# Three paired-attention stages: where unit weights are loaded, and the order of copies, exponentials and the closing projection

## The chip, the cores and the metric

One core of one Trainium2 chip runs the whole program in one launch. The metric is the device time in microseconds (us) of an execution; three executions of the kernel before took 2148.76, 2148.96 and 2149.0 us, so the median is 2148.96 us. The core has a matrix engine (TensorE, PE in the rows; its weight loads are PEld), VectorE (DVE), ScalarE (ACT), GpSimd (POOL) and SyncE (SP, which here only issues DMAs). Data lie in an on-chip memory of 128 partitions, matrix products land in eight PSUM banks of 128 x 512 floats.

## The reference

The reference runs two blocks on 512 tokens of width 1024, all in float32. The first is a layer norm, a gated mixer with two attentions, a norm, a mixture of 32 experts (top 4) and a norm. The second is a mixer of a sparse attention ("nsa"), a stick-breaking attention and a gated recurrence, then a norm. Three attentions matter here, cut to their core:

```python
# 1. differential attention, 4 heads, two score maps per head        (stage "diff")
s = einsum('bhqcd,bhkcd->cbhqk', q_blk, k);  p = softmax(where(allowed, s + alibi, -inf))
a = p[0] - lam * p[1];                       out = a @ v
# 2. chunk band attention, 8 heads with a relative bias                (stage "band")
p = softmax(where(valid, q_blk @ kb.T + bias, -inf));  out = p @ vb
# 3. nsa attention, 6 heads in 2 groups                                (stage "nsa")
p_c = masked_softmax(q @ kc.T * scale + bias_c)      # 31 compressed keys
p_s, p_w = ...                                       # selected blocks, and a window
out = g0 * (p_c @ vc) + g1 * (p_s @ vs) + g2 * (p_w @ vw)
```

Queries and keys come from products such as h @ w_in of 512 tokens by 1024 features.

## The kernel before, in words

The program is a row of stages with a barrier of all engines between them, so a stage that ends earlier moves all that follows. Three stages share one code, `heads_stage` (L638): "diff" (about 37 to 144 us of the span), "band" (174 to 268 us) and "nsa" (1779 to 1880 us).

A **unit** is a pair of score maps computed together: two halves m = 0, 1 of 64 feature rows each. diff and band have 4 units with 4 **items** each, one per block of 128 queries, with 128, 256, 384 and 512 keys. nsa has 3 units of 9 items: place 0 is the small item (31 compressed keys for all queries, 124 columns per half), then two items per query block (places 1 to 8: 128, 128, 256, 256, ... 512, 512 keys). Items are numbered t = 0, 1, ...; `items.place(t)` is the place in the unit and `items.closes(t)` marks the last place.

Every matrix is kept as a rounded upper part (a ScalarE cast, `upper_part`, L757) and a remainder (`split_lower`, L139), and a product takes three matmuls (L134 to L136). While unit u is worked on, the **projection** of unit u + 1 (queries and keys in diff and band, queries alone in nsa) is cut into pieces and spread over the items (`projection`, L724): 12 matmuls per item in diff and band, 3 per item at places 0 to 7 in nsa. In nsa, unit 0 is projected by the stage before.

For item t the engines run in lock step over semaphores. TensorE (L439): scores of t (L452), a share of the next projection, transposes of item t - 2 (L465, or L473 with the two halves apart), weighted values of item t - 3 (L487 or L492). VectorE (L498): scores plus bias with the row maximum (L511), then the normalisation of item t - 1 (L542 to L556), then at a closing item the copy of the next keys (`next_keys`, L803, L806), which a following unit's scores wait for. ScalarE (L570): exponentials of t (L582, L579 for the small item), the next queries' copy out of PSUM (`next_queries`, L776, L780), the copies of the transposed item t - 2 out of PSUM (L594 in diff, L599 in band and nsa), and then `weights`, the casts for a later unit. The copies free the banks that the next transposes write, half by half.

In nsa three more things are done beside. SyncE loads, first of all (`following`, L686), 2 MB of weights for the stick-breaking stage into `ahead`, then the query weights of unit 1 (`nsa_raw`) and of unit 2 (`nsa_q_raw`), two DMAs of 256 KB each with rows of 64 floats (L2125). ScalarE waits for unit 1's weights before it begins item 0 (L797). Four casts of `ahead` into `sb_up_qk` go out in units 1 and 2 (places 2 and 4, L774), and GpSimd takes their four remainders `ahead_lower` (L709); GpSimd also takes the remainders of the units' weights (L703) in all three stages.

## Time and profile before

| | |
|---|---|
| median of three executions | 2148.96 us |
| profiled execution | 2153.57 us |
| its span, first to last instruction | 2151.8 us |
| TensorE busy in the span | 90% |
| VectorE, ScalarE, GpSimd busy | 75%, 57%, 14% |
| first, second, third attention stretch (69 to 147, 188 to 270, 1780 to 1880 us) | TensorE busy 68.55 of 78, 74.49 of 82, 77.32 of 100 us |
| mean granted TensorE clock | 0.954 of full |

The profile is of one execution and has its own time; 1.8 us of it lie outside the span. In a row in order of time the first number is the start in us from the span's start, the second the length in us (of the whole group, where xN instructions stand in one row), and the brackets say how long the engine had been idle before it and what ended that. The middle of the span, about 430 to 1680 us, is the mixture of experts, which this change does not touch.

### The profile page before, as it was taken

To read this page: it belongs to the slowest core of one execution; us is meant where nothing else is said; L and a number is where in the kernel's file an instruction comes from. 1 tells how busy PE (TensorE), PEld (TensorE's weight loads), DVE (VectorE), ACT (ScalarE), POOL (GpSimd) and SP (SyncE) were. 2 spreads that over 40 slices of the span, in tenths; PEclk is the share of its full clock that TensorE was granted. 3 is DMA by queue.
4 is the path that set the end of the run, shared out by engine and by line. 5 is a ranking of instruction groups with operands and counts; after the bars stand their busy time and mean duration, and the time that the engine had idled before them with its cause. 6 is when DMAs were issued, how large, how long until landed. Compare 5 with 4: busy or idle time off the path is not lost. (4 is left out here: it accounts for less than half of the span.)

```text
span 2151.8 us, 28805 instructions
## 1 busy us (share of the span) xinstructions
PE 1945.5 (90%) x10052; PEld 1559.5 (72%) x10052; DVE 1610.0 (75%) x1815; ACT 1226.9 (57%) x1311; POOL 310.8 (14%) x176
## 2 busy tenths in 40 slices
PE   4988899974999999999999999999998497889998
PEld 3766678753788888888888888888886384576876
DVE  5363451457899999999999999999999434634786
ACT  3343532323677777777777777777776134642551
POOL 0202043101021212121111111111111000100000
PEclk9999999986999999999999999999999698999999
DMA  6222144445899999999999999999997352011122
GB/s 206 59 78 79 30 104 110 154 147 223 314 367 395 376 390 376 384 377 392 375 390 374 389 378 388 377 383 383 381 382 285 94 139 59 5 46 59 50 70 79
DMA packets 201612, 518.95 MB, mean 241 GB/s; under 512 B 21974, under 2 KB 81502, under 8 KB 201196
## 3 DMA queue, kind: packets, MB, share of 16 engines
q1 hardware_dynamic: 191212, 482.68, 60.3%
q0 software_dynamic: 9504, 34.61, 6.1%
q8 instruction: 41, 0.67, 0.1%
q10 hardware_dynamic: 832, 0.80, 0.1%
q14 instruction: 23, 0.19, 0.0%
HBM read 494.41 MB, written 29.41 MB: 243 GB/s over the span
## 5 line engine op out<-in xcount | busy, mean ns | idle before, releaser
L1759 ACT CAST moe_upper<-piece 128x2048 fp32r<-128x2048 f32 x384 | 734.1, 1914 | 284.7 <-PE bank L1691 270.1
L1839 DVE TENSOR_TENSOR piece_lower<-piece,moe_upper 128x2048 fp32r<-128x2048 f32 x384 | 870.1, 2286 | 30.0 <-ACT moe_upper L1759 30.0
L1689 PE MATMUL bank<-moe_upper,x_hi 128*128 128x512 f32 x1536 | 621.4, 405 | 2.5 <-DVE x_hi L1833 2.5
L1691 PE MATMUL bank<-moe_upper,x_hi 128*128 128x512 f32 x1536 | 607.1, 395 | 0.0
L1690 PE MATMUL bank<-piece_lower,x_hi 128*128 128x512 f32 x1536 | 602.5, 392 | 0.0
L1689 PEld LDWEIGHTS bank<-moe_upper,x_hi 128*128 128x128 f32 x1536 | 290.9, 189 | 67.8 <-DVE piece_lower L1839 2.9
L1690 PEld LDWEIGHTS bank<-piece_lower,x_hi 128*128 128x128 f32 x1536 | 290.7, 189 | 62.9
L1691 PEld LDWEIGHTS bank<-moe_upper,x_hi 128*128 128x128 f32 x1536 | 290.4, 189 | 62.6
L1643 POOL DMA_INDIRECT mixed<-moe_y,moe_dst x32 | 104.8, 3275 | 27.5 <-issue 27.5
L136 PE MATMUL bank<-x_hi,ahead_lower 128*128 128x512 f32 x256 | 102.1, 399 | 0.0
L1641 POOL COPY moe_dst<-row 128x1 uint32 (+1 forms) x32 | 6.9, 217 | 611.6 <-ACT moe_y L1748 611.6
L1633 POOL COPY moe_tok<-token 128x1 uint32 (+1 forms) x34 | 30.3, 890 | 341.5 <-DMA mixed<-moe_y,moe_dst 279.1
L1126 DVE TENSOR_TENSOR merge_tmp<-merge_sig,bank 128x512 f32<-128x512 f32 x8 | 5.5, 688 | 81.8 <-PE bank L136 81.5
L1635 POOL DMA_INDIRECT ahead<-h,moe_tok x34 | 61.0, 1795 | 32.5 <-issue 32.5
L300 PE MATMUL bank<-const,xs 128*128 128x128 f32 x96 | 20.3, 397 | 43.7 <-DVE xs L230 24.0
L136 PEld LDWEIGHTS bank<-x_hi,ahead_lower 128*128 128x128 f32 x256 | 49.3, 193 | 10.9
L135 PE MATMUL bank<-ahead_lower,x_hi 128*128 128x512 f32 (+1 forms) x140 | 55.8, 399 | 0.0
L134 PE MATMUL bank<-x_hi,merge_upper 128*128 128x512 f32 x128 | 50.6, 396 | 4.1 <-DVE ahead_lower L141 4.1
L300 PEld LDWEIGHTS bank<-const,xs 128*128 128x128 f32 x96 | 18.4, 213 | 47.8 <-DVE xs L230 44.8
L1828 DVE TENSOR_TENSOR moe_a<-moe_u,moe_sg 128x512 f32<-128x512 f32 x64 | 44.3, 693 | 10.6 <-issue 10.2
L135 PE MATMUL bank<-x_lo,merge_upper 128*128 128x512 f32 x128 | 50.4, 394 | 0.0
L1748 ACT ACTIVATE moe_y<-bank,slot_weight 128x512 f32<-128x512 f32 x64 | 40.2, 679 | 15.1 <-PE bank L1691 15.1
(571 smaller groups left out, 3051.5 us busy)
## 6 DMA issues: line engine op xcount, KB each, us to landing
piece<-in_w_exp_in_dram SPq DMA_DIRECT2D x256, 1024.0 KB, 7.7
piece<-in_w_exp_out_dram SPq DMA_DIRECT2D x128, 1024.0 KB, 9.6
ahead<-in_w_in_dram SPq DMA_DIRECT2D x19, 512.0 KB, 4.9
ahead<-in_w_in_dram SPq DMA_DIRECT2D x3, 2048.0 KB, 8.1
ahead<-in_w_in_dram SPq DMA_DIRECT2D x4, 1536.0 KB, 7.1
merge_raw<-in_w_in_dram SPq DMA_DIRECT2D x8, 512.0 KB, 5.5
ahead<-in_w_out_dram SPq DMA_DIRECT2D x2, 2048.0 KB, 7.9
out_w<-in_w_out_dram SPq DMA_DIRECT2D x2, 2048.0 KB, 8.3
```

The source lines that it names most:

```text
L134: nc.tensor.matmul(out, lhs.hi, rhs.hi, start=start, stop=False)
L135: nc.tensor.matmul(out, lhs.hi, rhs.lo, start=False, stop=False)
L136: return nc.tensor.matmul(out, lhs.lo, rhs.hi, start=False, stop=stop)
L1635: nc.gpsimd.indirect_dma_start(out=rows_in[p][:, :], out_offset=None, in_=k.h1[:, :], in_offset=bass.IndirectOffsetOnAxis(ap=tok[:, p:p + ...
L1643: nc.gpsimd.indirect_dma_start(out=k.mixed[:, :], out_offset=bass.IndirectOffsetOnAxis(ap=dst[:, 0:1], axis=0), in_=y[:, :], in_offset=Non ...
L1689: nc.tensor.matmul(to, hi[:, f, :], upper[u][:, t, cols], start=f == 0 and not biased, stop=False)
L1690: nc.tensor.matmul(to, hi[:, f, :], lower[s][:, t, cols], start=False, stop=False)
L1691: done = nc.tensor.matmul(to, lo[:, f, :], upper[u][:, t, cols], start=False, stop=f == NK - 1)
L1748: nc.scalar.activation(y[:, 512 * c:512 * c + 512], k.bank[4 + c][:, :], ACT.Copy, scale=r.slot_weight[:, ds(j, 1)]).then_inc(y_sb, 1)
L1759: nc.scalar.copy(upper[h % SPLIT][:, :, :], ring[s][:, :, :]).then_inc(hi_ready, 1)
L1828: nc.vector.tensor_tensor(a2[half][:, :], u2[half][:, :], sg2[half][:, :], ALU.mult) .then_inc(a_ready, 1)
L1839: nc.vector.tensor_tensor(lower[s][:, :, :], ring[s][:, :, :], upper[h % SPLIT][:, :, :].bitcast(F32), ALU.subtract).then_inc(lo_ready, 1)
```

## The change

It has eight parts.

1. TensorE: at a closing item the share of the next projection is issued ahead of the scores, not behind (diff and band; in nsa the closing place has no share).
2. VectorE: `next_keys` at a closing item stands ahead of that item's bias, not behind the normalisation.
3. ScalarE: for item t the copies of item t - 2 come first, then the next queries, then the exponentials, then `weights`.
4. nsa, SyncE: the query weights of unit 1 are loaded first, and `following` comes after them.
5. nsa, ScalarE: the cast of unit 1's weights is not waited for before item 0 but stands behind its exponential.
6. nsa, TensorE: the projection of unit 1 leaves places 0 and 1 free (`LATE = 2`) and has its 8 pieces at places 2 to 7, as 1, 1, 2, 1, 1, 2.
7. nsa: the four remainders `ahead_lower` are VectorE's, in units 1 and 2 at places 3 and 5, behind the normalisation.
8. GpSimd keeps the remainders of the units' weights alone.

```diff
 (attention_pe)
+            if items.closes(t):
+                projection(u + 1, items.place(t))
             if t >= 2:
                 pe.wait_ge(b["biased"], at + t - 1)
...
-            projection(u + 1, items.place(t))
+            if not items.closes(t):
+                projection(u + 1, items.place(t))
 (attention_dve)
+            if items.closes(t):
+                next_keys(u + 1)
             dve.wait_ge(b["scored"], at + t + 1)
...
-        if t < N and items.closes(t):
-            next_keys(items.unit(t) + 1)
+        if t < N:
+            other(items.unit(t), items.place(t))
 (attention_act: the block of the exponentials and next_queries moves behind the copies)
         if t < N:
+            next_queries(items.unit(t) + 1, items.place(t))
+            it = items.item(t)
+            e = b["e"][:, t % RING, :, 0:it["keys"]]
+            act.wait_ge(b["biased"], at + t + 1)
...
+            last.then_inc(b["exped"], 1)
             weights(items.unit(t) + 2, items.place(t))
 (heads_stage, sync)
-            if beside is not None:
-                following(sp)
             for u in range(done, units):
+                if beside is not None and u == 2:
+                    following(sp)
 (heads_stage, gpsimd)
-            if beside is not None:
-                for m in range(4):
...
-                    split_lower(nc.gpsimd, k.ahead[:, :, part], beside[:, :, part], k.ahead_lower[:, :, part])
 (heads_stage, tensor)
+                late = LATE if beside is not None and u == 1 else 0
+                step, steps = step - late, STEPS - late
+                if u < units and 0 <= step < steps:
+                    for n, c in PIECES[step * len(PIECES) // steps:(step + 1) * len(PIECES) // steps]:
                         project(u, n, c)
 (heads_stage, scalar)
             def weights(u, step):
+                if beside is not None and u == 2 and step == 0:
+                    upper_part(1, 0)
...
-            for n in range(projections):
-                upper_part(1, n)
+            if beside is None:
+                for n in range(projections):
+                    upper_part(1, n)
 (heads_stage, vector)
+            def remainders(u, step):
+                if beside is not None and u >= 1 and step in (3, 5):
+                    m = 2 * (u - 1) + (step - 3) // 2
+                    part = slice(P * m, P * m + P)
+                    dve.wait_ge(beside_hi, m + 1)
+                    split_lower(nc.vector, k.ahead[:, :, part], beside[:, :, part], k.ahead_lower[:, :, part])
```

What moves in the instruction order, at the three places that matter. Lines of the changed kernel are a few higher: L452 is L454 there, L465 is L468, L487 is L490, L582 is L603, L579 is L600, L599 is L592, L594 is L587, L780 is L783, L760 is L761, L2125 is L2136, L473 is L476, L556 is L561.

TensorE, diff, the closing item of unit 2 (scores 128x512) before: scores, then the first of the four pieces of unit 3's projection.

```order
L487 MATMUL bank<-v,diff_pt 128x128 [waits attention_copied]
L487 MATMUL bank<-v,diff_pt 128x128 x3
L452 MATMUL bank<-diff_heads_kt,diff_heads_q 128x512 [waits attention_biased]
L452 MATMUL bank<-diff_heads_kt,diff_heads_q 128x512
L134 MATMUL bank<-x_hi,v_upper 128x512
L135 MATMUL bank<-x_lo,v_upper 128x512
L136 MATMUL bank<-x_hi,ahead_lower 128x512
L134 MATMUL bank<-x_hi,v_upper 128x512
```

After: the end of the same projection, the scores, the transposes of item 9 and values of item 8 and the first scores of unit 3.

```order
L135 MATMUL bank<-x_lo,v_upper 128x512
L136 MATMUL bank<-x_hi,ahead_lower 128x512
L454 MATMUL bank<-diff_heads_kt,diff_heads_q 128x512 [waits attention_biased]
L454 MATMUL bank<-diff_heads_kt,diff_heads_q 128x512
L468 MATMUL bank<-const,diff_scores 128x128 [waits attention_copied,attention_normed]
L468 MATMUL bank<-const,diff_scores 128x128
L490 MATMUL bank<-v,diff_pt 128x128 [waits attention_out_copied,attention_copied]
L454 MATMUL bank<-diff_heads_kt,diff_heads_q 128x128 [waits attention_biased,units_evacuated]
```

The twelve projection matmuls are now ahead of the closing scores, and nothing long is left between those scores and the next unit's first ones.

SyncE at the start of nsa, before:

```order
L683 UNCONDITIONAL_BRANCH [waits barrier_Pool_Activation_PE_DVE_SP_release]
L310 DMA ahead<-in_w_in_dram 128x8x512
L2125 DMA nsa_raw<-in_w_in_dram 128x8x64 x2
L2125 DMA nsa_q_raw<-in_w_in_dram 128x8x64 [waits units_projected]
L2125 DMA nsa_q_raw<-in_w_in_dram 128x8x64
```

After:

```order
L687 UNCONDITIONAL_BRANCH [waits barrier_Pool_Activation_PE_DVE_SP_release]
L2136 DMA nsa_raw<-in_w_in_dram 128x8x64 x2
L310 DMA ahead<-in_w_in_dram 128x8x512
L2136 DMA nsa_q_raw<-in_w_in_dram 128x8x64 [waits units_projected]
L2136 DMA nsa_q_raw<-in_w_in_dram 128x8x64
```

The two DMAs of unit 1's weights now stand ahead of the 2 MB.

ScalarE at the start of nsa, before: items 0, 1 and 2, then the first copies.

```order
L780 ACTIVATE nsa_heads_q<-bank 128x512
L760 CAST nsa_upper<-nsa_raw 128x1024 [waits units_w1_in]
L579 ACT_TABLE_LOAD
L579 ACTIVATE nsa_scores<-nsa_scores 128x2x124 [waits attention_biased]
L582 ACTIVATE nsa_scores,nsa_l<-nsa_scores,nsa_nm 128x128 [waits attention_biased]
L582 ACTIVATE nsa_scores,nsa_l<-nsa_scores,nsa_nm 128x128
L582 ACTIVATE nsa_scores,nsa_l<-nsa_scores,nsa_nm 128x128 [waits attention_biased]
L582 ACTIVATE nsa_scores,nsa_l<-nsa_scores,nsa_nm 128x128
L599 COPY nsa_pt<-bank 31x512 [waits attention_transposed] x2
L582 ACTIVATE nsa_scores,nsa_l<-nsa_scores,nsa_nm 128x256 [waits attention_biased]
L582 ACTIVATE nsa_scores,nsa_l<-nsa_scores,nsa_nm 128x256
```

After:

```order
L783 ACTIVATE nsa_heads_q<-bank 128x512
L600 ACT_TABLE_LOAD
L600 ACTIVATE nsa_scores<-nsa_scores 128x2x124 [waits attention_biased]
L761 CAST nsa_upper<-nsa_raw 128x1024 [waits units_w1_in]
L603 ACTIVATE nsa_scores,nsa_l<-nsa_scores,nsa_nm 128x128 [waits attention_biased]
L603 ACTIVATE nsa_scores,nsa_l<-nsa_scores,nsa_nm 128x128
L592 COPY nsa_pt<-bank 31x512 [waits attention_transposed] x2
L603 ACTIVATE nsa_scores,nsa_l<-nsa_scores,nsa_nm 128x128 [waits attention_biased]
L603 ACTIVATE nsa_scores,nsa_l<-nsa_scores,nsa_nm 128x128
L592 COPY nsa_pt<-bank 128x128 [waits attention_transposed] x2
L603 ACTIVATE nsa_scores,nsa_l<-nsa_scores,nsa_nm 128x256 [waits attention_biased]
L603 ACTIVATE nsa_scores,nsa_l<-nsa_scores,nsa_nm 128x256
```

The cast that waits for the load (`units_w1_in`) has gone behind the first exponential, and each pair of copies is now ahead of the exponentials of the item two later.

## Rows read from the trace of the kernel before

**Rows 1.** Third attention stage, busy: PE, PEld, DVE, ACT, POOL; then clock, DMA share, GB/s.

```profile
1780.00:1880.00 100.00, 77.32 (x588) 50.04 (x588) 60.36 (x195) 58.28 (x166) 14.20 (x6) 0.90 0.12 32
```

**Rows 2.** Order of time, start of the third stage: start us, length us, engine, line.

```profile
1779.69 0.38 SPq L310 DMA_DIRECT2D ahead<-in_w_in_dram  x1
1780.13 4.44 SPq L2125 DMA_DIRECT2D nsa_raw<-in_w_in_dram  x2
1783.32 0.42 DVE L521 TENSOR_TENSOR nsa_scores<-nsa_scores,nsa_heads_small_m 128x248 f32<-128x248 f32 x1
1790.02 1.04 ACT L760 CAST nsa_upper<-nsa_raw 128x1024 fp32r<-128x1024 f32 x1 [9.70 <-DMA nsa_raw<-in_w_in_dram]
1791.15 2.34 POOL L141 TENSOR_TENSOR nsa_raw_lower<-nsa_raw,nsa_upper 128x1024 fp32r<-128x1024 f32 x1 [106.66 <-ACT nsa_upper L760]
1793.55 0.79 PE L134 MATMUL bank<-x_hi,nsa_upper 128*128 128x512 f32 x1 [11.25 <-POOL nsa_raw_lower L141]
1795.12 0.80 PE L452 MATMUL bank<-ks_t,nsa_heads_q 64*128 64x128 f32 x4
```

**Rows 3.** One tile, the query weights: issues (ns min/median/max) and landings.

```profile
L1966 SPq DMA_DIRECT2D nsa_q_raw<-in_w_in_dram x2: 1817/1898/1979, 1727.6 to 1729.7; - x2
DMA to landing us min/median/max: 4.3/6.0/6.2
```

**Rows 4.** Waits in the third stage: who for whom, us in total, times, longest.

```profile
PE bank L452 <- ACT nsa_heads_q L780: 5.4, 3, 2.3
PE bank L473 <- DVE nsa_scores L556: 3.5, 4, 1.8
PE bank L473 <- ACT nsa_pt L599: 2.7, 5, 1.2
```

**Rows 5.** Order of time, third stage: queries at a unit change, GpSimd beside VectorE.

```profile
1815.75 0.88 PE L492 MATMUL bank<-nsa_pt,vs 128*64 128x128 f32 x12
1817.57 0.57 ACT L780 ACTIVATE nsa_heads_q<-bank 128x512 f32<-128x512 f32 x1
1832.64 0.73 DVE L556 TENSOR_SCALAR nsa_scores<-nsa_scores,nsa_l,gates 128x256 f32<-128x256 f32 x2
1834.95 2.37 POOL L141 TENSOR_TENSOR ahead_lower<-ahead,sb_up_qk 128x1024 fp32r<-128x1024 f32 x1 [3.61 <-ACT sb_up_qk L774]
1835.22 2.57 DVE L556 TENSOR_SCALAR nsa_scores<-nsa_scores,nsa_l,gates 128x256 f32<-128x256 f32 x2
```

**Rows 6.** One line, the remainders on VectorE in the stage before: ns min/median/max.

```profile
L141 DVE TENSOR_TENSOR ahead_lower<-ahead,sb_up_qk x3: 1219/1220/1225, 1726.4 to 1728.7; 128x1024 fp32r<-128x1024 f32 x3
```

**Rows 7.** Waits in the first and in the second stage, as in rows 4.

```profile
PE bank L452 <- DVE diff_heads_kt L806: 2.6, 4, 1.0
...
PE bank L452 <- DVE band_heads_kt L806: 1.0, 2, 0.9
```

**Rows 8.** Order of time, first stage, change to its last unit.

```profile
124.12 0.50 PE L134 MATMUL bank<-x_hi,v_upper 128*128 128x512 f32 x1
124.24 0.69 DVE L511 CUSTOM_DVE_ANT_0 diff_scores<-bank,band_table 128x512 f32<-128x512 f32 x1 [0.31 <-PE bank L452]
126.28 0.62 DVE L548 SCALAR_TENSOR_TENSOR diff_scores<-diff_scores,diff_l 128x384 f32<-128x384 f32 x1
126.99 0.38 PE L465 MATMUL bank<-const,diff_scores 128*128 128x128 f32 x2
128.35 0.55 PE L465 MATMUL bank<-const,diff_scores 128*128 128x128 f32 x3
```

**Rows 9.** Order of time, end of the second stage.

```profile
259.28 0.72 ACT L582 ACTIVATE band_scores<-band_scores,band_nm 128x512 f32<-128x512 f32 x1 [2.04 <-DVE band_nm L511]
259.40 0.75 DVE L554 TENSOR_SCALAR band_scores<-band_scores,band_l 128x384 f32<-128x384 f32 x2
260.70 0.62 ACT L599 COPY band_pt<-bank 128x256 f32<-128x256 f32 x2
261.19 1.37 PE L473 MATMUL bank<-const,band_scores 128*128 128x128 f32 x6 [2.58 <-ACT band_pt L599]
```

More of the change, by code:

```diff
@@ L495, in attention_pe, with attention_dve @@
             last.then_inc(b["weighed"], 1)
-def attention_dve(nc, dve, k, items, b, next_keys, copy_out, ordered):
+def attention_dve(nc, dve, k, items, b, next_keys, copy_out, ordered, other):
     N, at = items.n, b["at"]
@@ L573, in attention_act @@
     for t in range(N + VALUE_LAG + 1):
-        if t < N:
-            it = items.item(t)
-            e = b["e"][:, t % RING, :, 0:it["keys"]]
-            act.wait_ge(b["biased"], at + t + 1)
-            if it["small"] is not None:
-                last = nc.scalar.activation(e, e, ACT.Exp)
-            else:
-                for m in range(2):
-                    last = nc.scalar.activation(e[:, m, :], e[:, m, :], ACT.Exp, bias=b["nm"][:, t % RING, m:m + 1],
-                                                scale=-1.0, accum_out=b["l"][:, t % RING, m:m + 1])
-            last.then_inc(b["exped"], 1)
-            next_queries(items.unit(t) + 1, items.place(t))
         n = t - TURN_LAG
@@ L601, in attention_act @@
         if t < N:
+            next_queries(items.unit(t) + 1, items.place(t))
+            it = items.item(t)
+            e = b["e"][:, t % RING, :, 0:it["keys"]]
+            act.wait_ge(b["biased"], at + t + 1)
+            if it["small"] is not None:
+                last = nc.scalar.activation(e, e, ACT.Exp)
+            else:
+                for m in range(2):
+                    last = nc.scalar.activation(e[:, m, :], e[:, m, :], ACT.Exp, bias=b["nm"][:, t % RING, m:m + 1],
+                                                scale=-1.0, accum_out=b["l"][:, t % RING, m:m + 1])
+            last.then_inc(b["exped"], 1)
             weights(items.unit(t) + 2, items.place(t))
@@ L632 @@
 UNIT_SEMS = ("w0_in", "w1_in", "w_hi", "w_split", "projected", "evacuated", "v_hi", "v_lo", "v_ps", "v_sb")
-FIRST_BANK = 3
+FIRST_BANK, LATE = 3, 2
 def heads_stage(nc, name, k, load, projections, items, values, q, copy_out, upper_out=None, keys=None, following=None,
@@ L724, in projection @@
             def projection(u, step):
-                if u < units and step < STEPS:
-                    for n, c in PIECES[step * len(PIECES) // STEPS:(step + 1) * len(PIECES) // STEPS]:
+                late = LATE if beside is not None and u == 1 else 0
+                step, steps = step - late, STEPS - late
+                if u < units and 0 <= step < steps:
+                    for n, c in PIECES[step * len(PIECES) // steps:(step + 1) * len(PIECES) // steps]:
                         project(u, n, c)
@@ L819, in _ @@
             next_keys(0)
-            attention_dve(nc, dve, k, items, b, next_keys, copy_out, keys is not None and upper_out is not None)
+            def remainders(u, step):
[4 more added lines that the diff above has]
+                    split_lower(nc.vector, k.ahead[:, :, part], beside[:, :, part], k.ahead_lower[:, :, part])
+            attention_dve(nc, dve, k, items, b, next_keys, copy_out, keys is not None and upper_out is not None, remainders)
     k.attention.counted(scored=items.n, out_copied=2 * units)
```

2 lines of the change are left out of this document (removed).

## The prediction

> **What bounds the kernel now.** I read the stretch of each attention stage first, since the change lies in these three alone, and barriers put whatever they gain or lose into the total. In the first two TensorE is busy for nine tenths of the time (the small table ahead), so they have little to give; in the third it is busy for 77.32 of 100 us [rows 1]. The order of time there shows one hole: TensorE ended the first scores at 1782.30 (1793.55 less the 11.25 in brackets) and stood until GpSimd's remainder of unit 1's weights was ready [rows 2]. Behind it is a chain: SyncE issued the 2 MB `ahead` first, then the two DMAs of `nsa_raw`; ScalarE waited for them until 1790.02 with nothing else done, cast for 1.04, GpSimd took 2.34. The waits of that stage name the rest: TensorE waited 5.4 us in three goes for the queries, 3.5 in four for VectorE's normalisation, 2.7 in five for ScalarE's copies of the transposes [rows 4]. In diff and band it waited 2.6 and 1.0 us for the copied keys [rows 7]. Elsewhere in these stages TensorE is the bound, so what is moved beside it costs nothing until it lets TensorE wait.
>
> **The load of unit 1's weights (parts 4 to 6).** The two DMAs now go out at the stage's start, 1779.7. In the stage before, an issue of this shape took 1.82 to 1.98 us, and the landings lay 4.3 to 6.2 us behind their issue [rows 3]. So the second goes out at 1781.6 and lands between 1785.9 and 1787.8. I take 1786.2, near the short end, because nothing stands ahead of it in its queue. ScalarE has by then the first exponential behind it (its input is ready at 1783.74, rows 2) and casts at once. Cast and remainder with their hand-overs took 3.53 us (1790.02 to 1793.55), so the projection can start at 1789.7, against 1793.55: 3.8 us sooner (2.2 to 4.1 by the landings; 0 if the load is no sooner at all). Meanwhile TensorE has computed the scores of items 1 and 2, which before came behind the hole: 0.80 for one [rows 2], and 0.5 to 0.8 for the other of the same shape. That is 1.3 us more. The `ahead` load moves behind by some 4 us, but it is wanted in unit 1 alone. TensorE restarts at its lower clock behind the hole either way (the stretch has 0.90 of full, rows 1); I count that as equal. The projection's pieces are as many as before, so spreading them differently is nothing by itself. The table load of the exponentials falls into ScalarE's wait. Term a: -3.8, term b: -1.3.
>
> **Queries ahead of the closing exponentials (part 3).** At the two later unit changes of nsa TensorE waits for a copy that is queued behind two exponentials of 512 keys. Of the 5.4 us, 2.3 belong to the stage's start and stay, so 3.1 are at stake [rows 4]. Now the copy stands behind ScalarE's second transposed copy (about 0.4 for 384 columns, of 0.31 for 256 in rows 9) and takes 0.57 itself, so it ends 1.0 us after the transposes, and TensorE has values of 0.88 us to do in that time [rows 5]. About 0.25 remain each time. Term c: -2.6 (-1.5 to -3.1).
>
> **Copies ahead of exponentials (part 3).** The end of band shows what this removes: two exponentials from 259.28 on, a copy behind them at 260.70, and transposes that had waited 2.58 us and began at 261.19, in the middle of that copy [rows 9]. In nsa such waits make 2.7 us, 1.2 of it one wait near the end. What is late next is the normalisation, ready some tenths earlier, so I take back 1.7 of the 2.7. Term d: -1.7 (0 to -2.7). The reverse side is that an exponential now waits for transposes. Where there is a projection, TensorE comes to the transposes late, so the exponential starts about 2 us later than now: in rows 8 the bias ends about 125.5 and the transposes follow at 126.99. Its result is wanted two items later, some 8 us, and the chain of copy, exponentials, next bias and normalisation is under 5 us. It costs nothing there; a rival below has the case that it does.
>
> **Remainders from GpSimd to VectorE (part 7).** VectorE's pair of 128x256 scalings took 0.73 us alone and 2.57 beside a GpSimd remainder, ending with it (1837.79 against 1837.32) [rows 5]: 1.84 lost. The remainder on VectorE itself takes 1.22 [rows 6]. Four times -0.62 is -2.5, but in unit 1 the loss is mostly hidden behind the projection, and of the 3.5 us that TensorE waited for the normalisation, one belongs to unit 0, beside the remainder of unit 2's own weights, and stays. Term e: -1.5, with +1.0 (the 1.22 shows where the loss did not) and -2.7 as ends. The Trainium skill, SBUF — State Buffer, section "Who interferes with whom", says that VectorE and GpSimd share a pair of ports by an exclusive lock, held for a whole instruction, and that a tensor_tensor with two on-chip inputs takes it too. By that rule all four losses are real and the new remainders, which meet no GpSimd work in units 1 and 2, run free: the sum would be 1.0 us lower. The trace agrees on the loss, not on who feels it, and I keep 1.5.
>
> **The closing projection and the keys (parts 1, 2).** Gain: the keys are copied while TensorE still has scores to do. Of 2.6 us in diff, the longest 1.0, some 0.9 is the first unit's copy, which nothing hides (band has the same 0.9 as its longest, rows 7), so 1.7 go; in band 0.1. Loss: into the last unit nothing covers VectorE's chain any longer. In rows 8, from the start of the closing bias (124.24) to the next-but-one transposes (128.35) were 4.1 us, of which the projection filled 2.87 (124.12 to 126.99) and the keys' wait 0.34 (2.6 less 0.9 and 1.0, over two), so 0.9 us are left to do. Yet the normalisation that those transposes need ends 2.66 us behind the start of that bias (126.90). TensorE stands for 1.8 us. Against before the transposes come 2.87 + 2.66 - 4.1 = 1.4 us later, and VectorE carries that to the end of the stage. In the earlier changes a new projection follows and hides it. Diff: -1.7 + 1.4 = -0.3, term f. Band loses a little less (1.1, shorter normalisations) and gets about as much back at its end, where the copy of rows 9 no longer holds the transposes (up to 1.04, from the normalisation's end at 260.15 to 261.19): 0, term g. Bounds for f and g together: -2 to +3, the upper one if band gets nothing back and GpSimd's moved remainders hit a normalisation.
>
> **Sum.** -3.8 - 1.3 - 2.6 - 1.7 - 1.5 - 0.3 = -11.2 us. The profiled execution took 2153.57 us (span 2151.8 and 1.8 around it) and would take 2142.4. It lies 4.6 above the median, which I take as constant: 2148.96 - 11.2 = 2137.8.
>
> **Rivals.**
> 1. *The load is no sooner.* The landing of `nsa_raw` may be set by its own many small pieces, or by `ahead` beside it, and not by its place in the queue; for it speaks that two more DMAs of this kind follow at once, against it that the same shape landed in 4.3 to 6.2 us [rows 3]. Then term a is 0: -7.4, 2141.6 us. The Trainium skill, DMA: Bandwidth & Descriptors, section "Specifications", puts the smallest piece at full rate at 512 B, and these rows are of 256 B. That rule favours this rival; no row here separates piece size from queue.
> 2. *The waits only change their name.* The stage's later half may be bound by VectorE as much as by TensorE, and c, d and e turn into waits for normalisations; for it speaks that VectorE is busy 60.36 of 100 us there, against it that the largest waits named are ScalarE's. Then -5.4: 2143.6 us.
> 3. *The closing order costs at every unit change.* If GpSimd's remainder, now later, falls on the normalisation next to each change, the four earlier ones pay 1.4 too: -5.6, 2143.4 us.
> 4. *Slower: exponentials behind transposes become the chain.* In the last units no projection stretches the period, an item of 512 keys takes TensorE about 2.7 us (an estimate: values 0.88 in rows 5, scores and transposes about as much each), and two of them, 5.4, must hold copies of 0.8, exponentials of 1.4 [rows 9] and a bias with normalisation of 2.66 [rows 8]. That is 4.9; it decides once hand-overs and the added remainders make more than 0.5 us. The eight or so items of 384 and 512 keys in the three last units would then each pay the 2 us shift of the exponentials: +17 against -11.2, 2155 us.
>
> **How the numbers follow.** Forecast 0.68, rival 1 0.10, rival 2 0.12, rival 3 0.06, rival 4 0.04. Time: 2137.8 us. The range runs from 2134.5 (landing at its best, c to e near their ends) to 2144.0, which takes in rivals 1 to 3. A measurement tells 0.2% (4.3 us) from no change. Faster is the forecast, rival 1 and about half to two thirds of 2 and 3, with small errors in mind: 0.87. Same 0.09, slower 0.04.
>
> **What the profile after would show.** Right: the cast of `nsa_raw` at 1786 to 1788 and a hole in TensorE of some 5 us that begins near 1784.5; waits for the queries of 0.2 to 0.4 at the later changes; no wait for `nsa_pt` over 0.4; no scaling of 2.5 us in units 1 and 2; no wait for keys after unit 0; a new wait of about 1.8 us for the normalisation at the last change in diff. Wrong: a landing at 1789 or later (a), waits for L556's successor that grow by what the copies' waits lose (d, e), waits for normalisations at changes that still have a projection (f).

## The result and the profile after

| | before | after |
|---|---|---|
| median, five executions each | 2148.96 us | 2136.11 us |
| profiled execution, span | 2153.57, 2151.8 us | 2135.08, 2133.2 us |
| mean granted TensorE clock of that execution | 0.954 | 0.958 |

The ratio after to before is 0.9939, with a 95% interval from 0.9929 to 0.9950: the change takes 12.85 us off the median (10.7 to 15.3 us by the interval). The prediction was 2137.8 us, with a range of 2134.5 to 2144.0.

The span can be cut at marks that both traces have: in diff and band from the first scores to the end of the last values, in nsa from the stage's first DMA to the end of its last values. Diff went from 68.66 to 68.32 us, band from 73.92 to 73.41, nsa from 99.66 to 86.65. That is 13.9 us against the 12.85 of the medians, so the gain lies in the three stages that the change touches. The two profiled executions differ by 18.6 us; the other 4.7 lie outside the three stages, about what the execution profiled before lies above the median (4.6).

First the third stage as a whole (columns as in [rows 1]; its clock is the third number from the end):

```profile
1774.92:1861.57 86.65, 76.70 (x588) 50.16 (x588) 58.57 (x198) 58.20 (x165) 4.70 (x2) 0.92 0.13 37
```

TensorE does the same 588 matmuls in 76.70 us (77.32 in [rows 1]). What went is idle time of TensorE: 22.3 us before, 9.95 after. The order of time at the stage's start, against [rows 2]:

```profile
1774.92 1.01 SPq L2136 DMA_DIRECT2D nsa_raw<-in_w_in_dram  x2
1775.97 0.92 SPq L310 DMA_DIRECT2D ahead<-in_w_in_dram  x1
1779.89 1.05 ACT L761 CAST nsa_upper<-nsa_raw 128x1024 fp32r<-128x1024 f32 x1 [0.48 <-DMA nsa_raw<-in_w_in_dram]
1781.02 2.34 POOL L141 TENSOR_TENSOR nsa_raw_lower<-nsa_raw,nsa_upper 128x1024 fp32r<-128x1024 f32 x1 [101.09 <-ACT nsa_upper L761]
1783.41 0.80 PE L134 MATMUL bank<-x_hi,nsa_upper 128*128 128x512 f32 x1 [3.60 <-POOL nsa_raw_lower L141]
```

The two small loads go out first, in 1.01 us where they took 4.44. The cast starts 4.97 us behind the stage's first DMA (10.33 before), and the projection 8.49 us behind it (13.86 before). TensorE waits 3.60 us there instead of 11.25. The waits of the stage, against [rows 4]:

```profile
PE bank L134 <- POOL nsa_raw_lower L141: 3.6, 1, 3.6
PE bank L454 <- ACT nsa_heads_q L783: 3.0, 3, 2.2
PE bank L476 <- DVE nsa_scores L561: 2.6, 5, 1.0
PE bank L495 <- ACT mixed_t L2145: 1.4, 2, 1.1
PE bank L454 <- DVE nsa_scores L526: 0.9, 1, 0.9
```

The wait for the queries is down from 5.4 to 3.0 us, of which 2.2 is the stage's start. The wait for ScalarE's transposed copies (2.7) is gone. The one for the normalisation went from 3.5 to 2.6, and 1.4 for the copy of the finished unit stands where 1.1 stood. The last row, 0.9, is new: the scores of item 2, which now come ahead of the weights, wait for the bias of item 0. These waits add up to the idle time that went: 7.65 at the weights less that 0.9, 2.4 for the queries, 2.7 for the copies, 0.9 for the normalisation, less 0.3 for the finished unit, 12.4 us in all. In diff and band, against [rows 7], then the change to diff's last unit and band's end, against [rows 8] and [rows 9]:

```profile
PE bank L454 <- DVE diff_heads_kt L810: 0.9, 1, 0.9
PE bank L468 <- DVE diff_scores L553: 4.1, 3, 2.0
...
PE bank L476 <- DVE band_scores L559: 2.5, 2, 1.6
```

```profile
124.69 0.69 DVE L516 CUSTOM_DVE_ANT_0 diff_scores<-bank,band_table 128x512 f32<-128x512 f32 x1 [0.38 <-PE bank L454]
126.72 0.62 DVE L553 SCALAR_TENSOR_TENSOR diff_scores<-diff_scores,diff_l 128x384 f32<-128x384 f32 x1
127.39 0.55 PE L468 MATMUL bank<-const,diff_scores 128*128 128x128 f32 x3 [1.74 <-DVE diff_scores L553]
...
258.50 0.75 DVE L559 TENSOR_SCALAR band_scores<-band_scores,band_l 128x384 f32<-128x384 f32 x2
259.30 1.01 PE L476 MATMUL bank<-const,band_scores 128*128 128x128 f32 x6 [1.59 <-DVE band_scores L559]
```

The keys are waited for once, by 0.9 us. In exchange TensorE waits 1.74 us for the normalisation at diff's last change. At band's end the 2.58 us for a copy have become 1.59 for a normalisation.

### The profile page after: what moved, and what is told of

It reads as the page before. It is cut to its first block and busy times, and to the rows that moved or that the text cites. A ratio compares the mean times of both kernels' runs of the same rounds, so it can differ in the third digit from the quotient of the medians.

```text
span 2133.2 us, 28805 instructions
## 1 busy us (share of the span) xinstructions
PE 1939.7 (91%) x10052; PEld 1553.1 (73%) x10052; DVE 1602.6 (75%) x1819; ACT 1226.0 (57%) x1311; POOL 296.6 (14%) x172
## 5 line engine op out<-in xcount | busy, mean ns | idle before, releaser
L1644 POOL COPY moe_tok<-token 128x1 uint32 (+1 forms) x34 | 24.8, 729 | 335.1 <-DMA mixed<-moe_y,moe_dst 273.7
L1833 DVE SCALAR_TENSOR_TENSOR moe_u<-moe_u,moe_g 128x512 f32<-128x512 f32 x64 | 44.3, 693 | 5.9
```

The lines of the kernel that those rows point to most:

```text
L1833: nc.vector.scalar_tensor_tensor(out=u2[half][:, :], in0=u2[half][:, :], scalar=1.0, in1=g2[half][:, :], op0=ALU.add, op1=ALU.mult)
```

## The experiments

All lengths in this table are read with the marks above; idle is the length less TensorE's busy time. Each ratio is to the kernel before on the same chip.

| kernel | ratio, 95% interval | diff | band | nsa | nsa busy, idle |
|---|---|---|---|---|---|
| before | 1 | 68.66 | 73.92 | 99.66 | 77.32, 22.3 |
| after | 0.9939, 0.9929 to 0.9950 | 68.32 | 73.41 | 86.65 | 76.70, 9.95 |
| a_again | 0.9929, 0.9916 to 0.9943 | 70.54 | 73.50 | 88.20 | 79.79, 8.4 |
| u_load | 0.9976, 0.9967 to 0.9985 | 68.43 | 73.36 | 94.84 | 78.33, 16.5 |
| u_scalar | 0.9993, 0.9984 to 1.0002 | 69.51 | 77.33 | 93.06 | 81.46, 11.6 |
| u_rem | 0.9952, 0.9939 to 0.9966 | 68.31 | 73.38 | 89.09 | 77.08, 12.0 |
| u_close | 0.9956, 0.9942 to 0.9970 | 71.90 | 76.18 | 85.52 | 76.87, 8.65 |
| o_scalar | 0.9994, 0.9985 to 1.0003 | 71.56 | 76.07 | 95.38 | 75.76, 19.6 |
| o_close | 1.0016, 1.0007 to 1.0025 | 68.19 | 77.28 | 99.57 | 77.29, 22.3 |
| two_q | 0.9963, 0.9951 to 0.9974 | 68.37 | 73.35 | 91.17 | 75.77, 15.4 |
| late0 | 0.9949, 0.9936 to 0.9963 | 68.31 | 73.38 | 88.96 | 78.03, 10.9 |
| o_load | 0.9969, 0.9958 to 0.9980 | 68.64 | 73.90 | 93.32 | 78.56, 14.8 |
| v1 | 0.9947, 0.9933 to 0.9960 | 68.44 | 73.36 | 84.49 | 76.01, 8.5 |
| v2 | 0.9939, 0.9925 to 0.9952 | 68.70 | 72.81 | 84.49 | 76.01, 8.5 |

**The same kernel again (a_again).**

> The changed kernel once more, unaltered, as the base for the kernels that undo one part. Theory: the gain lies in the third attention stage, so its length from the first DMA of the stage to the end of its last values is 86.6 us again (99.7 before), and the time is 0.9940 of the kernel before. Rival: part of the 12.85 us was a lucky placing of that one profile and set of runs (its runs spread over 2132 to 2141 us); then the ratio moves by more than 0.001 and the stage's length by more than 0.5 us.

The ratio agrees. The nsa stage was 1.55 us longer and diff 2.2, with the same instructions. Of the three traces whose nsa stage is the changed kernel's (u_close below alters no instruction there), the first, a_again and u_close differ in when TensorE ran at which of its two levels, 1.2 and 2.4 GHz (0.50 and 1.00 of full). The whole stage of a_again, and four stretches of it:

```profile
1780.23:1868.43 88.20, 79.79 (x588) 51.44 (x588) 59.61 (x198) 58.31 (x165) 4.70 (x2) 0.88 0.13 37
1792.00:1796.00 4.00, 4.00 (x17) 1.77 (x13) 1.45 (x7) 2.29 (x11) 0.00 (x0) 0.72 0.00 0
1844.00:1848.00 4.00, 2.98 (x30) 2.04 (x29) 3.06 (x15) 3.36 (x9) 0.00 (x0) 1.00 0.00 0
1848.00:1852.00 4.00, 3.88 (x16) 1.59 (x18) 2.75 (x10) 2.38 (x11) 0.00 (x0) 0.61 0.00 0
1852.00:1856.00 4.00, 4.00 (x16) 1.74 (x15) 2.76 (x9) 3.35 (x10) 0.00 (x0) 0.54 0.02 6
```

The first trace, whose stage starts 5.3 us earlier:

```profile
1786.00:1790.00 4.00, 4.00 (x16) 2.17 (x15) 1.46 (x7) 2.37 (x9) 0.00 (x0) 0.62 0.01 3
1790.00:1794.00 4.00, 4.00 (x24) 2.13 (x20) 1.59 (x7) 1.91 (x9) 0.00 (x0) 1.00 0.00 0
1842.00:1850.00 8.00, 6.67 (x45) 3.25 (x46) 7.31 (x24) 7.12 (x23) 0.00 (x0) 1.00 0.01 3
```

And of u_close:

```profile
1783.36:1868.88 85.52, 76.87 (x588) 50.12 (x588) 59.65 (x198) 58.49 (x165) 4.70 (x2) 0.92 0.13 38
1794.00:1798.00 4.00, 4.00 (x22) 1.85 (x20) 1.52 (x8) 3.18 (x12) 0.00 (x0) 0.95 0.05 11
```

If each mean is read as a part at 0.50 and the rest at 1.00, the full clock was back some 11 us behind the stage's start in u_close and 14 in the other two. In the last unit a_again ran about 7 of 8 us at the lower level (0.61, 0.54) and the first trace none (1.00); ahead of that fall TensorE had been busy 2.98 of 4 us at full clock. In u_close the lower level took some 3.4 us of the last unit. Against the first trace a_again has 3.1 us more of busy and 1.5 less of idle time, u_close 1.3 less of idle time. The same instructions thus take 85.5, 86.7 or 88.2 us, and the clock differs with them. The times follow: the five executions of a_again were 2140.7, 2138.3, 2136.7, 2133.9 and 2132.1 us at mean clocks of 0.954, 0.956, 0.956, 0.959 and 0.961. The rival's ±0.5 us for a single trace was too narrow; single traces are compared below by their waits where they differ by less than 2 us.

**The load undone (u_load) and alone (o_load).** The first puts `following(sp)` back ahead of all loads, `upper_part(1, n)` back ahead of the attention, and LATE to 0; the second makes only these three edits in the kernel before.

```diff
+            if beside is not None:
+                following(sp)
             for u in range(done, units):
-                if beside is not None and u == 2:
-                    following(sp)
-FIRST_BANK, LATE = 3, 2
+FIRST_BANK, LATE = 3, 0
```

> The changed kernel with the load of unit 1's weights as before: the 2 MB load ahead of the two small ones, the cast of unit 1's weights at the stage's start, the projection from step 0. Theory (terms a and b, with the landing as measured): the third stage gets 5.1 to 6.5 us longer, all of it ahead of the first scores of item 9, and the first small load is issued over 4 us again. Rival: the start only moves a wait; with ScalarE's new order, the later waits absorb part of it, and the stage gets longer by 3 us or less. Time by the theory 5 to 6.5 us over the changed kernel, by the rival 3 or less.

> The kernel before with the load of unit 1's weights alone (parts 4 to 6). Theory: terms a and b with the landing as measured, 5.4 to 5.9 for the projection's start and 1.3 for the scores: the third stage 92.5 to 93 us (99.66 before), diff and band as before, 6 to 7 us faster, ratio 0.997. Rival A (the parts are not additive here either): 4 us or less. Rival B: the full 8 us that its undoing cost in the changed kernel.

Undone, nsa is 6.6 to 9.3 us longer than in the three traces, and 6.3 to 8.1 us of it are there by the first scores of unit 1: TensorE waits 11.41 us for the weights. The median is 8.1 us above that of a_again on the same chip (2144.73 against 2136.66), more than the 5 to 6.5 that I expected. Alone, it takes 6.3 us off nsa and nothing off diff and band, with the projection 8.29 us behind the stage's start. The ratio says 6.7 us, as expected (4.3 to 9.0 by its interval). So the rivals of 3 and of 4 us or less are out. Between 6.7 alone and 8.1 undone the noise does not let me tell; it is near to additive.

**ScalarE's order undone (u_scalar) and alone (o_scalar).**

```diff
+        if t < N:
+            it = items.item(t)
...
+            last.then_inc(b["exped"], 1)
+            next_queries(items.unit(t) + 1, items.place(t))
         n = t - TURN_LAG
...
         if t < N:
-            next_queries(items.unit(t) + 1, items.place(t))
-            it = items.item(t)
...
-            last.then_inc(b["exped"], 1)
```

> The changed kernel with ScalarE's order as before: exponentials, then the queries, then the copies of the transposes. Theory (terms c and d): the two waits for the queries are 1.57 us again and the waits for the copies come back, +4.3 us in the third stage; and about 1 us at band's end, where the last transposes wait behind exponentials and a copy. So 4.3 to 5.3 us over the changed kernel. Rival (the waits only change their name): the stage's second half is bound by VectorE as much, waits for normalisations shrink as the others grow, and it costs 2 us or less. Second rival: it costs more than 6 us, because the two orders decide how far TensorE runs ahead of VectorE.

> The kernel before with ScalarE's new order alone (queries ahead, copies ahead of exponentials). Undoing this part in the changed kernel cost 12.6 us, while the prediction's terms c and d give 4.3 us in nsa. Theory X (the two orders fit together: without the copies ahead, the closing projection makes band's new wait of 1.9 us and its end of 2.6): alone it brings 4.3 us in nsa and 2.0 to 2.6 at band's end, 6 to 7 us in all. Rival Y (it is additive, and the terms were undersized by three): 12 us faster than before. Rival Z (a gap that goes moves the clock: a part of the 12.6 was TensorE at its lower clock): the third stage shortens by 3 to 4 us and the number of stretches at the lower clock decides the rest, 3 to 8 us.

Here the number of u_scalar's second rival came: undone, the part costs nearly the whole gain (12.6 us by the medians). Of the 11.5 us that the three stages show, diff has 1.2, band 3.9 and nsa 6.4. In nsa the waits for queries and copies come back (5.0 us), but those for the normalisation fall from 2.6 to 0.2, so idle time grows by 1.65 us against the first trace and 3.2 against a_again; the rest is the clock. The first rival (waits that change their name) is thus half true there.

Alone, it brings nothing that can be told. Nsa is 4.3 us shorter (95.38 against 99.66), the number of terms c and d, but only 2.7 of it is idle time (19.6 against 22.3); the rest is the same matmuls in 75.76 us where they took 77.32, at a mean clock of 0.91 where it was 0.90. The waits for queries and copies fell by 4.9 us, and those for the normalisation grew by 2.1 (3.5 to 5.5). The longest, 2.27 us, is also in u_rem below (2.28), and 0.8 in the changed kernel: it comes with the remainders on GpSimd. And diff gets 2.9 us longer and band 2.15. None of my theories had that. The change to diff's second unit in o_scalar shows it:

```profile
87.15 1.04 ACT L763 CAST diff_upper<-diff_raw 128x1024 fp32r<-128x1024 f32 x1
88.27 2.39 POOL L141 TENSOR_TENSOR diff_raw_lower<-diff_raw,diff_upper 128x1024 fp32r<-128x1024 f32 x1 [13.44 <-ACT diff_upper L763]
88.33 2.55 DVE L546 TENSOR_SCALAR diff_scores<-diff_scores,diff_l 128x384 f32<-128x384 f32 x1
91.49 0.68 DVE L809 COPY diff_heads_kt<-bank 128x512 f32<-128x512 f32 x1
92.23 0.49 PE L452 MATMUL bank<-diff_heads_kt,diff_heads_q 64*128 64x128 f32 x4 [2.08 <-DVE diff_heads_kt L809]
```

The exponentials wait for the transposes, which stand behind the closing projection, so the cast behind them comes late (87.15; it was 85.68 in the kernel before, whose scores began 0.2 us sooner). GpSimd's remainder then starts at 88.27, just ahead of VectorE's scaling, which takes 2.55 us where 0.42 is usual. The copy of the keys stands behind that, and TensorE waits 2.08. In the changed kernel the same place reads:

```profile
87.07 2.36 POOL L141 TENSOR_TENSOR diff_raw_lower<-diff_raw,diff_upper 128x1024 fp32r<-128x1024 f32 x1 [13.41 <-ACT diff_upper L761]
87.27 0.69 DVE L810 COPY diff_heads_kt<-bank 128x512 f32<-128x512 f32 x1 [3.61 <-PE bank L136]
88.34 0.69 DVE L516 CUSTOM_DVE_ANT_0 diff_scores<-bank,band_table 128x512 f32<-128x512 f32 x1 [0.38 <-PE bank L454]
89.88 0.42 DVE L551 TENSOR_SCALAR diff_scores<-diff_scores,diff_l 128x384 f32<-128x384 f32 x1
```

The keys are copied at 87.27, beside the remainder, and the scaling comes behind it (89.88, 0.42 us).

**The closing order undone (u_close) and alone (o_close).**

```diff
-            if items.closes(t):
-                projection(u + 1, items.place(t))
...
-            if not items.closes(t):
-                projection(u + 1, items.place(t))
+            projection(u + 1, items.place(t))
```

(and `next_keys` behind the normalisation again)

> The changed kernel with the closing projection behind its scores and the copy of the keys behind the normalisation again, ScalarE's new order kept. Theory (terms f and g): the keys' waits come back (+1.7 us in diff, 0.1 in band) and the new waits at the change into the last unit go (1.73 in diff, 0.94 in band): 0.3 us in diff, 0 to -0.9 in band, so a time within 1 us of the changed kernel. Rival A (the closing order is a loss that ScalarE's order only covers): 1.5 to 3 us faster than the changed kernel, most of it in band. Rival B (the closing order is what the gain of ScalarE's new order needs): over 2 us slower.

> The kernel before with the closing projection and the keys alone (parts 1 and 2). The prediction's terms f and g: 0.3 us faster, no change that can be told. Theory X (it fits only with ScalarE's new order): band gets 1.9 us longer by a wait for the copy of the transposes at the change into the last unit, as with ScalarE's order undone, diff is equal, so 2 to 4 us slower than before. Rival: equal within 1 us, if the 1.9 us wait came from something else in that kernel.

Undone, diff is 3.6 and band 2.8 us longer than in the first trace (waits for the keys 4.6 and 3.0 us): rival B. The times point the same way, 3.7 to 5.8 us over the changed kernel, with intervals that overlap at the edges. Alone, it makes the kernel 0.16% slower (about 3.4 us), as theory X had it: band is 3.4 us longer, 1.8 of it idle time. Its change to the last unit, and the stretch behind it (columns as in [rows 1]):

```profile
247.84 0.72 ACT L587 ACTIVATE band_scores<-band_scores,band_nm 128x512 f32<-128x512 f32 x1 [4.78 <-DVE band_nm L516]
248.56 0.70 ACT L587 ACTIVATE band_scores<-band_scores,band_nm 128x512 f32<-128x512 f32 x1
249.27 0.62 ACT L604 COPY band_pt<-bank 128x256 f32<-128x256 f32 x2
249.76 0.57 PE L476 MATMUL bank<-const,band_scores 128*128 128x128 f32 x2 [1.93 <-ACT band_pt L604]
...
249.77:253.77 4.00, 4.00 (x22) 2.69 (x23) 1.08 (x3) 1.81 (x7) 0.00 (x0) 0.57 0.67 174
```

With no projection between scores and transposes any more, the transposes come up while ScalarE has two exponentials ahead of the copy that frees their bank, and wait 1.93 us. Right behind that wait the granted clock is 0.57, most of it at the lower level, where the kernels before and after have 1.00. Band's same matmuls take 1.6 us more (mean clock 0.956 against 0.977), and so they do, within 0.1 us, in u_scalar, which has the same wait.

So neither order gains alone over the whole kernel, and together diff and band lose nothing (0.85 us shorter in the first trace, where ScalarE's order alone has them 5.1 us longer and the closing order alone 2.9): the closing order takes the keys and the normalisation out of the remainder's way, ScalarE's order takes the copy out from behind the exponentials. The two orders without the other parts were not run, so what the pair gains by itself is not shown.

**The remainders on GpSimd (u_rem).** `split_lower(nc.vector, ...)` back to a loop of `split_lower(nc.gpsimd, ...)` behind the unit's own.

> The changed kernel with the four remainders of the parked weights on GpSimd again, directly behind the remainder of the unit's own weights. Theory (term e): pairs of scalings of 2.5 us stand again in units 1 and 2 and the third stage is 1.5 us longer. Rival A (each of the four costs VectorE its whole 1.84 less 1.22): 2.5 us longer. Rival B (VectorE has room there once ScalarE's copies come first): no change within 0.5 us, or up to 1 us shorter, since VectorE is freed of 4 x 1.22 us.

Nsa is 2.4 us longer than in the first trace (2.1 by idle time, at the same clock of 0.92). The first trace is the one to compare with, since the clock changed at the same places in both. Unit 1, from its first scores to those of unit 2, took 27.7 us where it took 26.8 in all three traces; unit 2 took 30.4 where it took 28.8 in the first. TensorE's waits for the normalisation are 4.9 us against 2.6. Two of the four, with VectorE's scalings beside them:

```profile
1817.55 2.35 POOL L141 TENSOR_TENSOR ahead_lower<-ahead,sb_up_qk 128x1024 fp32r<-128x1024 f32 x1 [14.28 <-ACT sb_up_qk L782]
1817.78 2.46 DVE L561 TENSOR_SCALAR nsa_scores<-nsa_scores,nsa_l,gates 128x128 f32<-128x128 f32 x2
1823.32 2.38 POOL L141 TENSOR_TENSOR ahead_lower<-ahead,sb_up_qk 128x1024 fp32r<-128x1024 f32 x1 [3.42 <-ACT sb_up_qk L782]
1823.37 2.80 DVE L561 TENSOR_SCALAR nsa_scores<-nsa_scores,nsa_l,gates 128x256 f32<-128x256 f32 x2
```

All four scalings of units 1 and 2 that meet a remainder take 2.45 us or more. In the changed kernel the remainder is VectorE's and takes what [rows 6] said:

```profile
1818.27 1.22 DVE L141 TENSOR_TENSOR ahead_lower<-ahead,sb_up_qk 128x1024 fp32r<-128x1024 f32 x1
```

The times give 3 us over the changed kernel (0.9952 against 0.9929 and 0.9939, intervals overlapping). Rival A, near its 2.5.

**Two queues (two_q).** `following(act)` at the start of ScalarE's program, `following(sp)` out of SyncE's.

> The changed kernel with the 2 MB load issued by ScalarE at the stage's start, so that it stands in another queue, beside the two small loads of SyncE and not behind them. Theory (place in the queue): the small loads are issued in 1.0 us and land 5.0 us after the stage's start as in the changed kernel; same time within 1 us. Rival (the DMA engines are shared: whoever is beside the 2 MB load is late): issue still short but the landing at 8 to 10 us, and the time 3 to 5 us longer. Second rival: the issue itself takes over 4 us again although the queue is empty, because what holds it is common to both queues.

```profile
1775.65 1.01 SPq L2136 DMA_DIRECT2D nsa_raw<-in_w_in_dram  x2
1775.67 0.47 ACTq L310 DMA_DIRECT2D ahead<-in_w_in_dram  x1
1776.71 6.65 SPq L2136 DMA_DIRECT2D nsa_q_raw<-in_w_in_dram  x2
1786.09 1.04 ACT L759 CAST nsa_upper<-nsa_raw 128x1024 fp32r<-128x1024 f32 x1 [5.44 <-DMA nsa_raw<-in_w_in_dram]
```

The issue is short, as theory and rival both had it; the landing is not. The cast starts 10.44 us behind the stage's start, as before (10.33), and nsa is 3.0 to 5.7 us longer than in the three traces (5.2 to 7.3 us by the ratios). Median us from issue to landing are the last number of these rows, for before, after and two_q:

```profile
nsa_raw<-in_w_in_dram SPq DMA_DIRECT2D x2, 256.0 KB, 9.1
```

```profile
nsa_raw<-in_w_in_dram SPq DMA_DIRECT2D x2, 256.0 KB, 3.9
```

```profile
nsa_raw<-in_w_in_dram SPq DMA_DIRECT2D x2, 256.0 KB, 8.5
```

One small load was issued with the large one and the other half a us later. So a queue of its own does not help small loads that go out at the same moment as the large one. In the changed kernel the 2 MB are on their way too, but were issued 1.05 us behind the first small load and in its queue; whether that head start or the order in the queue protects the small loads, no run separates. The 4.44 us that SyncE spent on the small issues in the kernel before are not the cause of the late landing: with them gone it is as late. Nor does a long issue need the 2 MB in the same queue: here the next pair of small loads, unit 2's `nsa_q_raw`, took 6.65 us to issue in SyncE's queue, with only two small loads ahead of it there.

**From step 0 (late0).** `LATE = 0`, the load still first.

> The changed kernel with the projection of unit 1 spread from step 0 on (LATE = 0), the small load still first. Theory (term b): TensorE waits for the weights directly behind the scores of item 0, and the scores of items 1 and 2 come behind the hole, so the third stage gets 1.3 us longer. Rival: no change within 0.5 us, since VectorE and ScalarE, which those scores feed, are waited for later anyway. Second rival: more than 1.3, since items 1 and 2 are then biased and normalised only behind the projection's first pieces. The same third stage took 85.5, 86.7 and 88.2 us in three traces in which its instructions were the same, so a difference under 1.5 us in one trace tells nothing; the waits are what is compared.

TensorE waits 5.46 us for the weights where it waited 3.0 to 3.6. Nsa is 88.96 us; the ratios differ by 0.001 to 0.002, with overlapping intervals. The waits say that term b is there (1.9 to 2.5 us of wait, some of it given back). So does the stretch from the stage's start to the first scores of unit 1: 32.6 us against 31.05 in the first trace and 30.6 in a_again, with the clock back at 14 us in all three. That is 1.6 to 2.0 us, somewhat more than the 1.3 of the theory. The times alone do not show it.

**A shorter start (v1) and a split closing order (v2).**

```diff
-                    upper_part(1, 0)
+                    nc.scalar.copy(upper[1][:, 0, 0:4, :], raw[1][:, 0, 0:4, :]).then_inc(half_hi, 1)
+                    nc.scalar.copy(upper[1][:, 0, 4:8, :], raw[1][:, 0, 4:8, :]).then_inc(w_hi, 1)
...
+                if beside is not None and u == 0 and step == 1:
+                    dve.wait_ge(half_hi, 1)
+                    split_lower(nc.vector, raw[1][:, 0, 0:4, :], upper[1][:, 0, 0:4, :],
+                                lower[1][:, 0, 0:4, :]).then_inc(half_lo, 1)
...
```

> The changed kernel with the weights of nsa's unit 1 cast by ScalarE in two halves and their remainders taken by VectorE in two halves, ahead of the normalisation of item 1, in place of GpSimd's one of 2.34 us. Theory (chain at the stage's start: landing, cast, remainder, projection): cast 0.55 and remainder 0.65 for the first half, so the projection starts 1.7 us sooner, and VectorE's scaling of item 1 (1.71 us beside GpSimd) takes 0.6: 1.7 to 2.7 us off the third stage. Rival: VectorE is late by the 1.3 us of the two remainders, the bias of item 2 and the normalisations behind it come later, and the wait moves there: under 0.5 us.

```profile
1780.95 0.62 ACT L773 CAST nsa_upper<-nsa_raw 128x512 fp32r<-128x512 f32 x1 [0.49 <-DMA nsa_raw<-in_w_in_dram]
1781.93 1.29 DVE L141 TENSOR_TENSOR nsa_raw_lower<-nsa_raw,nsa_upper 128x512 fp32r<-128x512 f32 x2
1782.66 0.80 PE L134 MATMUL bank<-x_hi,nsa_upper 128*128 128x512 f32 x1 [1.79 <-DVE nsa_raw_lower L141]
```

```profile
1775.98:1860.47 84.49, 76.01 (x588) 49.70 (x588) 58.56 (x200) 58.29 (x166) 2.37 (x1) 0.94 0.13 38
```

The projection starts 6.68 us behind the stage's start, 1.2 to 1.8 sooner, and nsa is 84.49 us in v1 and in v2: shorter than each of the three traces. The start is as the theory has it. The gain is not: the clock was back 11 us behind the stage's start, as in u_close, and against that trace the first scores of unit 1 come 0.8 us sooner (28.5 against 29.3), while the waits for the normalisation are 2.9 us against 1.8, as the rival has it in part. The times show no gain. The ratio of v1 is 0.9947, of the changed kernel 0.9939 and 0.9929. I do not call it faster.

v2 adds `and u + 2 < items.units` to the closing condition.

> The same, and the closing projection and the copy of the keys go ahead only at changes that another projection follows; at the change into the last unit they stand as in the kernel before. Theory (the runs with the closing order undone had a wait of 1.0 for the normalisation and 0.34 for the keys there, the changed kernel 1.74): 0.4 us off diff, nothing in band (0.28 and 0.76 against 0.94). Too little for the times to tell from the kernel without it; the waits of diff tell. Rival: the longer wait at that change shielded what follows, and a wait of the same size comes behind it.

In diff the waits are 1.0, 2.0 and 0.8 us for the normalisation and 0.3 for the keys beyond the first, against 1.74, 0.33 and 2.0: the rival came, and diff (68.70) is no shorter. Band is 0.6 us shorter than the first trace. In the times v2 equals the changed kernel; no version beat it.

## Why the prediction was right

**Term a was mis-sized: -3.8 predicted, -5.4 measured.** The step was "I take 1786.2", 6.5 us behind the first issue, from issues of 1.9 us and landings of 4.3 to 6.2 [rows 3]. Two issues into an empty queue took 1.01 us together, and the cast began 4.97 us behind the first. The changed kernel's projection started 5.4 to 6.0 us sooner in the three traces, o_load's 5.6, all outside the bounds of 2.2 to 4.1. Reason and sign held; the issue time came from rows with a backlog, three other loads issued in the 2.3 us ahead of them.

**Term b, -1.3, held in kind.** late0 gives 1.9 to 2.5 us of wait and 1.6 to 2.0 of length; o_load's 6.3 us for a and b together is what -5.4 and about -1 make.

**Terms c and d, -4.3: c was right, d cannot be told from e, and their price in diff and band was wrong.** The waits for the queries are 0.37 each (0.25 forecast), so c is -2.4. The copies' 2.7 us are gone, the normalisation's waits are down by 0.9, and the finished unit's are up by 0.3: 3.3 for d and e together, where 3.2 was forecast. That o_scalar's nsa is 4.3 us shorter, to the tenth the sum of c and d, is luck: 2.7 of it is idle time and 1.55 the clock. But the sentence that exponentials behind transposes cost "nothing there" in diff and band holds only because the closing order stands beside them. Without it they cost 5.1 us.

**Term e: -1.5 predicted, -2.1 to -2.4 by the traces.** I held that in unit 1 the loss hides behind the projection; u_rem shows it mostly does not: VectorE's scalings met all four remainders, and unit 1 was 0.9 us longer where two whole losses make 1.24. Unit 2 was 1.6 us longer. The Trainium skill, SBUF — State Buffer, section "Who interferes with whom", has the rule of an exclusive lock, and the sum by it was 1.0 us lower than mine. The stretched scalings (2.46 to 2.80 us a pair) agree with the rule, and the run lies nearer to the rule.

**Terms f and g were right as sums.** Diff: -0.3 predicted, -0.34 measured, the new wait 1.74 where 1.8 was forecast, and one for the keys, at unit 0 alone. The agreement to a few hundredths is luck: idle time in diff is the same (4.7 us), and a_again's diff is 2.2 us longer. Band: 0 predicted, -0.5 measured: 0.94 us new at the change, 1.0 given back at the end. As the price of the closing order they were wrong: by itself it costs 2.9 us over diff and band.

**The rivals.** Rival 1 (load no sooner) is out by the trace. Its reason was half right: two_q shows that `ahead` beside the small loads does delay them, but in the changed kernel it is issued behind both. The small pieces did not make the load late; the median landing was 3.9 us with rows of 256 B. The Trainium skill, DMA: Bandwidth & Descriptors, section "Specifications", has 512 B as the smallest piece at full rate; the landing came sooner with rows of 256 B all the same, and no run here varies the piece. Rival 2 is out for the whole change, since idle time in nsa fell by 12.4 us and the waits for the normalisation with it; for ScalarE's order alone it is half true (o_scalar: 4.9 us of waits gone, 2.1 come back). Rival 3 did not come at the changes of the changed kernel, yet its mechanism, GpSimd's remainder on the closing normalisation, is what o_scalar ran into. Rival 4 did not come.

**The sum.** The median moved 1.65 us further than forecast. Term a alone was 1.6 us too small in size; c, d and e made 5.7 us of waits where 5.8 were forecast. That the median came so near is in part luck, since the terms left out the clock: nsa's length varies by 2.7 us with no instruction changed. In u_scalar nsa is 6.4 us longer than in the first trace, only 1.65 of it idle time; the other 4.8 are the same matmuls, more of them at the lower level. Whether u_scalar's order brings this on, or chance, one trace can't tell.

What stays open: why the changed kernel's executions spread over 9 us and those of the kernel before over 5. The clock goes with it in a_again, but no run here sets what the clock does.

## What to carry to other kernels

A reordering on one engine that delays anything another engine is paced by (here a cast, and by it a GpSimd remainder) has to be priced at the places where that other work lands, stage by stage. Two orders that each cost time in some stages when alone can cost nothing there together, so undo each part and do each part alone before calling one useless. Of loads that are wanted at different times, issue the urgent small one first: here, putting the large one in another queue at the same moment left the small one as late as behind it.

## What the runs showed of the hardware

- Two 256 KB loads in 256 B rows took 1.01 us to issue into an empty queue, 4.44 us behind a 2 MB load, and 6.65 us behind two such small loads with the 2 MB in another queue (two_q). The long issue did not set the landing: 10.33 us behind the stage's start with it, 10.44 without it but with the 2 MB load in flight, 4.97 with that load behind.
- Beside a GpSimd remainder, VectorE's tensor_scalar out of on-chip memory took 2.55 us instead of 0.42, while a copy of the keys out of a PSUM bank (0.69) and the bias op (0.69) ran at their usual length beside the one at 87.07 to 89.43.
- Right behind a wait of 1.93 us of TensorE in band (o_close, 249.76) the granted clock was 0.57 for 4 us; without the wait it was 1.00 there.
- The same nsa instructions took 85.5, 86.7 and 88.2 us; the return to full clock came 11 to 14 us behind the stage's start, behind the same hole of 3.0 to 3.6 us.
